# Depthwise convolution of a hybrid decoder: its third and fourth channel group made of ScalarE products that GpSimd adds

## What is computed

```python
def conformer_conv(u, w_dw, b_dw, ln_g, ln_b, w_out):
    a, g = jnp.split(u, 2, axis=-1)
    y = a * jax.nn.sigmoid(g)
    y = lax.conv_general_dilated(
        y, w_dw[:, None, :].astype(y.dtype), window_strides=(1,),
        padding=((CONV_WIDTH - 1, 0),),
        dimension_numbers=('NWC', 'WIO', 'NWC'),
        feature_group_count=CONV_DIM) + b_dw
    y = jax.nn.silu(layer_norm(y, ln_g, ln_b))
    return y @ w_out
```

## Time and profile before

| | us |
|---|---|
| median of 3 runs | 1933.04 |
| lowest, highest | 1932.81, 1936.19 |
| the profiled execution | 1936.59 |
| its span on the core | 1934.3 |
| PE busy, mean clock granted to PE | 1824.0, 0.976 of full |

### The profile page before, as it was taken

One profiled execution on the slowest core, in us unless ns is written; L12 is line 12 of the kernel. 1 busy time (PEld: TensorE's weight loads), 2 busy tenths in 40 slices (PEclk: granted clock), 3 DMA queues, 4 the chain that ended last, 5 costly groups with the idle time before them and its releaser, 6 DMA issues.

```text
span 1934.3 us, 29139 instructions
## 1 busy us (share of the span) xinstructions
PE 1824.0 (94%) x10820; PEld 1595.9 (83%) x10821; DVE 1553.7 (80%) x1414; ACT 1129.3 (58%) x952; POOL 190.9 (10%) x156
## 2 busy tenths in 40 slices
PE   2999997899979999979999999999999999999997
PEld 2989997899969999877887787787877877878776
DVE  6998776999557667767888888888888888888886
ACT  4444564433354554645776767667767676677674
POOL 0394001000007800100000000000000000000000
PEclk7999999999989999989999999999999999999999
DMA  9965443799525333434988989979889899898892
GB/s 365 348 230 207 155 149 132 267 372 375 207 87 178 128 131 133 152 131 181 364 338 330 368 300 363 365 303 365 333 332 366 301 362 366 304 366 332 332 365 80
DMA packets 72524, 525.33 MB, mean 272 GB/s; under 512 B 8112, under 2 KB 8240, under 8 KB 8704
## 3 DMA queue, kind: packets, MB, share of 16 engines
q1 hardware_dynamic: 72288, 524.03, 72.0%
q0 software_dynamic: 160, 0.23, 0.0%
HBM read 523.17 MB, written 1.05 MB: 271 GB/s over the span
## 4 chain that ended last, share of the span: by engine, by line
PE 44%; DVE 9%; ACT 3%; issue 2%; DVEq 0%; ACTq 0%
PE bank L1591 24%; PE bank L1606 12%; DVE w_lo L1101 7%; ACT w_hi L728 3%; PE bank L1616 2%; PE bank L1626 2%; PE bank L1644 2%; PE bank L1333 1%; DVE arena L1235 1%; PE bank L1310 1%; PE bank L1561 0%; DVE arena L895 0%; DVE arena L917 0%; DVE arena L921 0%; DVEq L1233 0%
## 5 line engine op out<-in xcount | busy, mean ns | idle before, releaser
L1101 DVE TENSOR_TENSOR w_lo<-raw,w_hi 128x2048 fp32r<-128x2048 f32 x224 | 512.9, 2290 | 85.9 <-ACT w_hi L728 64.1
L728 ACT ACTIVATE w_hi<-raw 128x2048 fp32r<-128x2048 f32 x224 | 428.4, 1916 | 126.2 <-PE bank L1606 77.0
L1333 PE MATMUL bank<-acts,w_hi 128*128 128x256 f32 x2080 | 378.8, 286 | 37.3 <-DVE acts L908 30.7
L1333 PEld LDWEIGHTS bank<-acts,w_hi 128*128 128x128 f32 x2080 | 326.8, 194 | 41.2 <-issue 33.0
L1591 PE MATMUL bank<-acts 128*128 128x512 f32 x1248 | 305.1, 393 | 0.0
L1591 PE MATMUL bank<-w_hi,acts 128*128 128x512 f32 x960 | 300.4, 394 | 1.3 <-DVE acts L1247 1.3
L1333 PE MATMUL bank<-acts,w_lo 128*128 128x256 f32 x1040 | 295.2, 284 | 0.0
L1101 DVE TENSOR_TENSOR acts<-raw,acts 128x2048 fp32r<-128x2048 f32 x112 | 256.3, 2289 | 32.4 <-ACT acts L728 29.0
L1591 PEld LDWEIGHTS bank<-acts 128*128 128x128 f32 x1248 | 233.6, 188 | 52.9
L1606 PE MATMUL bank<-w_hi,acts 128*128 128x512 f32 x832 | 263.1, 397 | 0.0
L728 ACT ACTIVATE acts<-raw 128x2048 fp32r<-128x2048 f32 x112 | 214.8, 1917 | 72.9 <-PE bank L1591 70.5
(11 more groups left out here) (229 smaller groups left out, 2120.3 us busy)
## 6 DMA issues: line engine op xcount, KB each, us to landing
raw<-in_experts SPq DMA_DIRECT2D x336, 1024.0 KB, 4.8
raw<-in_stream SPq DMA_DIRECT2D x161, 1024.0 KB, 5.6
arena<-in_x_t SPq DMA_DIRECT2D x1, 1024.0 KB, 11.8
out_t<-arena SPq DMA_DIRECT2D x2, 512.0 KB, 2.6
arena<-in_c_row SPq DMA_DIRECT2D x1, 512.0 KB, 4.3
arena<-in_vecs SPq DMA_DIRECT2D x1, 224.0 KB, 2.7
arena<-in_glr_w POOLq DMA_DIRECT2D x2, 64.0 KB, 4.1
arena<-in_a POOLq DMA_DIRECT2D x2, 32.0 KB, 4.3
```

Of the source, the lines that this page charges most:

```text
L728: act.activation(w_hi[s], raw[:, slot, :], ACT.Copy).then_inc(hi_written, 1)
L1101: dve.tensor_tensor(w_lo[s], raw[:, slot, :], f32(w_hi[s]), ALU.subtract).then_inc(lo_written, 1)
L1333: mm = pe.matmul(out[:, c, :], w[:, 256 * k + P * c:256 * k + P * c + P], (hi if high else lo)[:, k, :], start=(k == 0 and n == 0 and c == 0),
```

## The change

ACT now multiplies the shifted tiles of groups 2 and 3 with their weights (`multiply_taps`, 62 instructions per layer, at steps 6 to 25, three or four a step; the first one of each group adds the bias and goes straight to `conv_acc`). POOL only adds: 60 additions per layer out of four rows of `conv_tmp`, in the order in which ACT makes the products. DVE keeps groups 0 and 1. An ACT product waits for the addition that last read its row.

```diff
-        pool_products = sem("pool_conv_products")
+        act_products = sem("act_conv_products")
...
-            def taps(layer, k0, k1):
-
-                for k in range(k0, k1):
-                    w = vec(layer, "conv_dw")[:, TAPS * 3 + k:TAPS * 3 + k + 1]
-                    src, acc, product = ypad[:, 3, k:k + T], conv_acc[:, 3, :], conv_tmp[:, k % 2, :]
-                    if k == 0:
-                        pool.tensor_scalar(acc, src, w, vec(layer, "conv_dw_b")[:, 3:4],
-                                           ALU.mult, ALU.add).then_inc(pool_taps, 1)
-                        continue
-                    if k > 1:
-                        pool.wait_ge(pool_taps, TAPS * layer + k - 1)
-                    pool.tensor_scalar(product, src, w, None, ALU.mult).then_inc(pool_products, 1)
-                    products[0] += 1
-                    pool.wait_ge(pool_products, products[0])
-                    pool.wait_ge(pool_taps, TAPS * layer + k)
-                    pool.tensor_tensor(acc, acc, product, ALU.add).then_inc(pool_taps, 1)
+            def add_products(layer):
+
+                for n in range(2, 2 * TAPS):
+                    acc = conv_acc[:, 2 + n % 2, :]
+                    pool.wait_ge(act_products, 2 * TAPS * layer + n + 1)
+                    if n >= 4:
+                        pool.wait_ge(pool_taps, (2 * TAPS - 2) * layer + n - 3)
+                    pool.tensor_tensor(acc, acc, conv_tmp[:, (n - 2) % 4, :], ALU.add).then_inc(pool_taps, 1)
...
-                wait_read(pool, ("z", layer, 3, 0))
-                taps(layer, 0, TAPS)
+                add_products(layer)
...
+            def multiply_taps(layer, n0, n1):
+
+                for n in range(n0, n1):
+                    k, c = divmod(n, 2)
+                    w = vec(layer, "conv_dw")[:, TAPS * (2 + c) + k:TAPS * (2 + c) + k + 1]
+                    src = ypad[:, 2 + c, k:k + T]
+                    if k == 0:
+                        act.activation(conv_acc[:, 2 + c, :], src, ACT.Identity, scale=w,
+                                       bias=vec(layer, "conv_dw_b")[:, 2 + c:3 + c]).then_inc(act_products, 1)
+                        continue
+                    if n >= 6:
+                        act.wait_ge(pool_taps, (2 * TAPS - 2) * layer + n - 5)
+                    act.activation(conv_tmp[:, (n - 2) % 4, :], src, ACT.Copy, scale=w).then_inc(act_products, 1)
...
+                if i == 6:
+                    wait_read(act, ("z", layer, 3, 0))
+                if 6 <= i < 26:
+                    multiply_taps(layer, 2 * TAPS * (i - 6) // 20, 2 * TAPS * (i - 5) // 20)
...
-                    for c in range(3):
-                        first = (4, 4, 6)[c]
+                    for c in range(2):
+                        first = 4
...
-                pe.wait_ge(pool_taps, TAPS * (layer + 1))
+                pe.wait_ge(pool_taps, (2 * TAPS - 2) * (layer + 1))
```

More of the change, by code:

```diff
@@ L462, in _ @@
             pool.affine_select(one_or_zero[:, :], ones, [[-1, P]], ALU.is_equal, 0.0, 0, 1).then_inc(mask_written, 1)
-            products = [0]
-            def taps(layer, k0, k1):
-                for k in range(k0, k1):
-                    w = vec(layer, "conv_dw")[:, TAPS * 3 + k:TAPS * 3 + k + 1]
-                    src, acc, product = ypad[:, 3, k:k + T], conv_acc[:, 3, :], conv_tmp[:, k % 2, :]
-                    if k == 0:
-                        pool.tensor_scalar(acc, src, w, vec(layer, "conv_dw_b")[:, 3:4],
-                                           ALU.mult, ALU.add).then_inc(pool_taps, 1)
-                        continue
-                    if k > 1:
-                        pool.wait_ge(pool_taps, TAPS * layer + k - 1)
-                    pool.tensor_scalar(product, src, w, None, ALU.mult).then_inc(pool_products, 1)
-                    products[0] += 1
-                    pool.wait_ge(pool_products, products[0])
-                    pool.wait_ge(pool_taps, TAPS * layer + k)
-                    pool.tensor_tensor(acc, acc, product, ALU.add).then_inc(pool_taps, 1)
+            def add_products(layer):
[5 more added lines that the diff above has]
+                    pool.tensor_tensor(acc, acc, conv_tmp[:, (n - 2) % 4, :], ALU.add).then_inc(pool_taps, 1)
             for layer in range(DEPTH):
```

## The result

The changed kernel takes **1947.78 us** (median of 15 runs, 1937.48 to 1950.56) against 1933.68 us of the kernel before (15 runs, 1932.62 to 1936.19). The ratio is 1.0065, its 95% interval 1.0053 to 1.0078: slower by 10 to 15 us. The forecast was 1936.1 us, 3.1 us above the kernel before, with a range up to 1941.0 us. The direction was right and the size was not: the change costs 14.1 us, and its time lies 6.8 us beyond the range. The profiled execution took 1949.17 us, 12.6 more than the one before, and its span is 1947.2 us.

A forecast was written before the change was run, and what follows sets the result against it. PE, busy 94% of the span, was taken as the bound, with DVE limiting early in layer 0 and before `gla_out`; +0.7 early and +1.2 late per layer gave +3.1 on 1933.04: 1936.1 us, range 1928.5 to 1941.0.

The forecast's parts named there:

- Part 2: Early, layer 0 around unit 10: POOL's products go, additions come in threes; low part 0.9 us earlier, slow matmuls 1.6: +0.7 us.
- Part 4: ACT, steps 6 to 25: 62 more products per layer, 1.2 us a step, covered by its idle time; nothing counted.
- Part 5: New waits: ACT's products for POOL's additions free in time; POOL's mask ready near 230 us, cover about 1 us.
- The signs named for the case "right": POOL additions 0.7 to 2.5 us, DVE rows drawn out, unit 10 near 106.7, `gla_out` waiting 2 us or more, ACT unhindered.
- part 3: Late, between scans and states: 11 additions add 4.7 us, seven taps and select collision go; `gla_out` +1.2 us per layer.
- The bounds: Additions costing DVE nothing to 0.60 us each: total -6.6 to +8.9 us; late place at most +3.0 per layer.
- the slow matmuls: 0 or 1.6 us: Bound on PE's double-spaced matmuls after its early wait near unit 10: either no cost or 1.6 us.
- The third: Rival: each POOL addition blocks DVE for its whole 0.73 us; unit 10 at 110.6; +13.6 us, 1946.7; chance 0.03.
- The second: Rival: each addition hits DVE at its worst, 0.55 to 0.60 us, so states and L991 bound PE; +7 to +9; chance 0.17.
- The first: Rival: additions mostly fall into DVE's gaps, 0.2 us each; -6.2 us, 1926.8; chance 0.2.
- the last: Rival: DVE's relief and new delays cancel, slow matmuls do not follow; +1.5 us or less, 1933 to 1934.5; chance 0.13.
- The fourth: Rival: ACT held by POOL at steps 22 to 25, up to 2.4 us per layer; +7.9 us, 1940.9; chance 0.07.

The follow-up runs named there:

- e1: Changed kernel with each of POOL's 120 additions replaced by a memset of the row it wrote, output incomplete: 1924.82 us, ratio 0.9959.
- e2: Changed kernel with 24 extra matmuls on PE ahead of `gla_out`'s wait for the states in each layer: 1937.72 us, ratio 1.0019.
- e3: Kernel before, with two unused reciprocals on DVE ahead of the GLA states in each layer: 1947.0 us, ratio 1.0074.
- e10: Kernel before, with two unused DVE reciprocals ahead of the states and 24 extra matmuls on PE ahead of `gla_out`'s wait: 1938.81 us, ratio 1.0027.
- e6: Changed kernel with ACT's products, and POOL's additions behind them, at steps 11 to 25 only: 1947.8 us, ratio 1.0079.
- e9: Kernel before, with one unused 128x128 reciprocal on DVE ahead of the GLA states in each layer: 1942.94 us, ratio 1.0053.
- e11: Changed kernel, but ACT multiplies group 3 only, POOL adds 30 times a layer and DVE keeps group 2: 1946.64 us, ratio 1.0066.
- e5: Changed kernel with ACT's products, and POOL's additions behind them, at steps 6 to 20 only: 1931.83 us, ratio 0.9991.
- e4: Changed kernel with ACT's products, and POOL's additions behind them, at steps 11 to 20 only: 1927.41 us, ratio 0.9976.
- e7: Kernel before with DVE's 31 taps of group 2 per layer left out, output incomplete: 1927.73 us, ratio 0.9972.
- e8: Changed kernel with products at steps 11 to 20 only, those of step 20 behind ACT's softplus input (`log_a`): 1926.14 us, ratio 0.9968.

## Why the prediction was wrong

**Right, by its own steps.** *Part 2*: unit 10 was put at 106.7 us after a wait of 2.8 and started at 107.01 after 2.82. Its low part ended at 106.95, by part 2's own sum 0.45 us per addition where 0.43 was taken. Slow matmuls followed the wait, as assumed; they lasted 6 us instead of 3.2, and the place came out at +2.0 instead of +0.7. *Part 4*: e1 shows ACT's products at no cost. *Part 5*: no wait of ACT for POOL, and the mask in time. The signs named for the case "right" appeared (but for POOL's longest additions, 2.79 us where 2.5 was named), and still the time was 11.7 us off: none of them looked at PE's clock behind `gla_out`.

**The step that failed is part 3, the price of the late place: "+1.2 us in each layer".** It has two errors, a small one and the large one.

- The wait: 11 additions at 0.43 were counted. 13 met the chain, at 0.48, so `gla_out`'s wait grew by 3.77 - 1.54 = 2.2 us and 2.95 - 0.87 = 2.1, instead of 1.2.
- What follows the wait: nothing was counted. Measured, 15.04 - 10.32 = 4.7 us in each layer, at a granted clock of 0.50. e2 takes it away and gives back 10.1 us; e3 makes it with no change of POOL. Together with the wait the place costs about 6.9 us a layer and not 1.2.

The prediction had this effect in hand. The earlier trace rows show it behind a wait of 1.87 us, and part 2 priced it for unit 10; part 3 then had `gla_out` wait 1.54 + 1.2 = 2.7 us and 2.1 us, both longer than 1.87, and did not ask the same question there. With 4.7 us a layer added the sum would have been +12.5 us, 1945.5. The bounds had the same hole: their upper end for the late place, +3.0, was waiting alone, so that the range ended at 1941.0. The sentence "the slow matmuls: 0 or 1.6 us" rested on one observation and was applied to the early place alone. Waits of that length are followed by slow matmuls in some runs and not in others (last section), so 0 was possible, but the upper end had to hold `gla_out` too.

The page "TensorE: Matmul & The Clock Gate" of the Trainium skill says of this (Part 1) that "the default state is throttled, and activity releases the throttle". e2 and e10 agree: with work in the wait, whose results nobody uses, the granted clock stays at 1.00 in the stretch behind it.

**The rivals.** The third ("the whole addition blocks", 1946.7) names nearly the measured time, by a mechanism that the trace denies: additions cost 0.48, not 0.73, and unit 10 started at 107.0, not at 110.6. The second was in the right place with too small a price. The first, and the last ("moves nothing that PE sees"), are out: `gla_out` waits longer in both layers. The fourth did not occur.

The sum by the measured terms, from PE's timeline: +2.0 at attention; +4.3 at `gla_out` and +9.1 at `gla_sums` of layer 0 (249.52 - 240.46); +11.8 and +16.5 in layer 1. The end of the span is at +12.9, so 3.6 us come back behind the second mixer; what gives them back was not followed.

## What to carry to other kernels

A wait of PE that grows must be priced twice, for its length and for the clock behind it: wherever the trace shows one wait followed by slow matmuls, the sum or at least its upper bound must charge them to every wait that a change makes as long. A place where they did not follow is no safe bound. GpSimd's additions are free only while DVE has slack: moved off the steps that feed PE's waits, the same 120 additions turned +14 us into -8.4. And a gain ahead of a wait for another engine was worth nothing here (e6): shorten the last chain first.

## What the runs showed of the hardware

- **The price of a wait jumps.** Waits of 1.54 and 0.87 us had the clock at 1.00 behind them, those of 2.5 and 2.4 us in e9 cost 1.6 and 3.3 us on top, those of 2.95 to 4.3 us between 2.8 (e11, layer 1) and 4.8 us: 0.95 us of delay, twice, came to 9.6.
- **The length of the wait alone does not decide.** Of the waits between 1.7 and 2.3 us, slow matmuls followed 1.74 and 1.86 (e5), 1.83 (e4), 1.87 (before), 1.98 (e7) and 2.24 (e3), and did not follow 1.97 (e3), 1.98 and 2.24 (e9) or 2.27 (e8). The two of e9, with the clock at 1.00 from 107 to 113 us:

```profile
99.22 0.50 PE L1347 MATMUL bank<-w_hi,acts 128*128 128x256 f32 x2 [1.98 <-DVE w_lo L850]
...
107.38 0.50 PE L1334 MATMUL bank<-acts,w_hi 128*128 128x256 f32 x2 [2.24 <-DVE w_lo L850]
```

- **It differs between executions of the same code.** Up to unit 10 the kernel before, e3 and e9 run the same instructions; the clock granted from 100 to 107 us and from 107 to 113 us was 0.76 and 1.00 in the first, 1.00 and 0.72 in e3, 1.00 and 1.00 in e9. The changed kernel's runs spread over 13 us; its two shortest (1937.48 and 1937.65 us) had a mean clock of 0.979 and the length of e2, the others 0.969 to 0.976. That these two kept their clock at `gla_out` is likely, but neither of them was profiled.
- **24 matmuls (3.04 us) in the wait pay for themselves**: about 5 us a layer in e2, 4 in e10.
